# Two usual pairs in place of four ahead of the up projection's seven-product loop

## The chip, the cores and the metric

The kernel runs on one core of a Trainium2 chip. The metric is the device time of one execution in microseconds; lower is better. TensorE (PE) multiplies matrices, VectorE (DVE), ScalarE (ACT) and GpSimd (POOL) do the elementwise work, SyncE (SP) starts most of the transfers. Each engine runs its own instructions in the order written; semaphores connect them.

## The reference

One transformer block and a second one of two layers, for one sequence of 1024 tokens and width 1024. The change lies in the feed-forward part of the first block alone:

```
h2 = rms_norm(x, norm2_g)
up = h2 @ w_up                      # 1024 -> 2 * 2816
up = causal_depthwise_conv(up, ffn_dw_w)     # width 3
gate, val = split(up, 2)
x = x + (silu(gate) * val) @ w_down
```

The 2816 channels are 22 tiles of 128. A tile of the gate and the tile of the value that goes with it are called a pair: 22 pairs, each with 1024 x 256 weights.

## The kernel before

Activations lie transposed, channels on the 128 partitions. A (8 tiles of 128 x 1024, f32) is the normed input of the up projection. TensorE multiplies in a reduced 32-bit type, so each factor is split in a high part (a copy in that type) and a low part (the rest), and each product is three matmuls: high by high, high by low, low by high (lines 253 to 255, 2012 to 2014).

**Usual pairs** (`up_first_pe`, line 1986; UP_FIRST = 4 of them, numbers 0 to 3). `dense_unit` multiplies the unit's weights (WH, WL, 128 x 2048) with the halves HH, HL of the input: 8 row tiles x 2 (gate, value) x 2 halves of the tokens x 3 = 96 matmuls of 512 columns. Pairs 0 and 2 go to the PSUM banks PB, pairs 1 and 3 to TBB and OBB. The input isn't normed by tokens yet, so DVE scales the result by rbx (`scaled`, L2146), then come the copies with the last tap (ScalarE, L2098 and L2100, into G0 and V0), the other taps (`taps_of`, DVE, L2081), silu (ScalarE) and the product gate by value (DVE, L2158), which SP stores to `ub`. The unit's low part is a DVE subtraction (`low_part`, L269), its high part a GpSimd transfer (L3244).

**Pairs in seven products** (`up_pe`, line 1999; pairs 4 to 21). A pair's product is cut in 2 x 2 quarters: weights by row half and gate or value, input by row half and token half. Seven products of sums of quarters (M0 to M6), 4 row tiles x 3 = 12 matmuls each, replace eight: 84 matmuls. For them the kernel needs

- seven *mixes* of the input, made once: sums on GpSimd (mixes 2, 4, 6; `mixed`, L2211, four operations each) or DVE (3 and 5; `mix_sum`, L2055), each with a high part (ScalarE, `mix_high`, L2048) and a low part (DVE, `mix_low`, L2060). They lie in XH and XL; mixes 3 to 6 lie over HH and HL, so they wait until the last usual pair has read these (marks h1, h3, h5 and the pair's end);
- seven *pieces* of each pair's weights: sums on GpSimd (0 to 3 and 6; `piece_sum`, L2203), high parts on ScalarE (`piece_high`, L2066), low parts on DVE (`piece_low`, L2072). Raw weights come by SP (`up`, L2515) to RAW and RAW1 by turns; RAW1 shares memory with rbx;
- combinations of the seven results: m2, a ScalarE copy of M0 (L2126 or L2258), which product 4 waits for; q, r and others on DVE (L2190, L2314). Product 5 waits for q, product 6 for r.

The pairs run as `ffn_up0` (two pairs, 4 and 5, written out), `ffn_up` (a loop of two pairs a round, UP_LOOPS rounds) and `ffn_up_last` (20 and 21). The work that readies pair 4 lies in `up_first_act`, `up_first_dve` and `up_pool`, woven into that of the usual pairs. In `up_first_dve` the order is: mix 0 and 1 low, pair 0, mix 2 low, pairs 1 and 2 with a split each, then sum for mix 3, pieces 0 to 3, sum for mix 5, mix 3 low, scaling of pair 3, mix 4 low, pieces 4 and 5, mix 5 low, q, mix 6 low, r, piece 6, taps of pair 3; then in `up_dve` pieces 0 to 3 of pair 5.

The product that begins a pair waits for its piece 0, and the first pair's for its mixes too:

```
if j:
    pe.e.wait_ge(dve_done, at_mark(pe, "dve", f"w{p}_0", i))
else:
    pe.e.wait_ge(dve_done, at_prev(pe, "dve", f"w{p}_1", i))
    if ph == UP_PHASES[0]:
        pe.e.wait_ge(dve_done, done_in("dve", "ffn_first", f"x{p}"))
```

Beside the loop, 16 *gained* units go through ScalarE: SP loads a unit of later weights to gs (L2559), ScalarE multiplies it by gains (`gain_unit`, L2240, 16 operations), SP stores it to `gu` (L2549). Before, these go with pairs 5 to 20.

Of the kernel before, what the change touches and what calls it, by code (L numbers as in the profile page):

```python
# [41 lines left out]
DIFF_HEADS = 8  # L42
# [27 lines left out]
U_FFN = U_WO + 4  # L70
UP_FIRST = 4
U_DOWN = U_FFN + UP_FIRST
# [11 lines left out]
def build(nc, io, counts, stop=None):  # L84

    made = {"pe": {}, "act": {}, "dve": {}}
    with ExitStack() as ctx:
# [1998 lines left out]
        def up_first_act(act):  # L2086
            e = act.e
# [20 lines left out]
            for p in range(3):  # L2108
                mix_high(act, p)
            for j in range(3):  # L2110
                gate_value(j)
                silu(j)
# [4 lines left out]
            mix_high(act, 4)  # L2117
            e.wait_ge(pe_done, at_mark(act, "pe", "v3"))
            for p in (4, 5):
                piece_high(act, p, 1, UP_FIRST)  # L2120
            mix_high(act, 5)
            gate_value(3)
            e.wait_ge(dve_done, at_mark(act, "dve", "x1"))
# [7 lines left out]
        def up_first_dve(dve):  # L2131
# [33 lines left out]
            mix_low(dve, 2)  # L2165
            low_part(dve, U_FFN + 2)
            scaled(1)
            taps_of(1)
            product(1)
            low_part(dve, U_FFN + 3)  # L2170
            scaled(2)
            taps_of(2)
            product(2)
            mix_sum(dve, 3, "h1")
# [3 lines left out]
            mix_low(dve, 3)  # L2178
            scaled(3)
            mix_low(dve, 4)  # L2180
# [16 lines left out]
            combined("ra_f", 3, "r_f", rb[:, 0, :], rb[:, 0, :], ALU.add)  # L2197
            taps_of(3)

# [5 lines left out]
        def up_pool(pool, high):  # L2205
# [9 lines left out]
            mixed(2)  # L2215
            for n in (U_FFN + 2, U_FFN + 3):
                high(n, 0, io["units"][n:n + 1])
            pool.wait_ge(raw_up[0], 16)
            pool.wait_ge(pe_done, done_in("pe", "ffn_first", "v2"))
            for p in range(4):  # L2220
                piece_sum(pool, p, UP_FIRST)
            for p, name in ((4, "h3"), (6, "v3")):
                pool.wait_ge(pe_done, done_in("pe", "ffn_first", name))
                mixed(p)
# [7 lines left out]
        def up_act(act, ph):  # L2232
            e = act.e

            def gain_unit(j, i):

                e.wait_ge(gain_in, counted(act, i, 32, 16 * j))
                for n in range(2 * KT):
                    part = gs[:, n * P:(n + 1) * P]
                    ins = e.activation(part, part, ACT.Copy, scale=p_(("pre_b", "kvn")[n // KT], n % KT, 1))  # L2240
                ins.then_inc(act_done, act.mark(f"gain_{j}"))

            def body(i):
                for j in range(2):
# [14 lines left out]
                    if build:  # L2259
                        for p in range(3):  # L2260
                            high(p)
                        if first:
                            e.wait_ge(dve_done, done_in("dve", "ffn_first", f"cg_{tag(UP_FIRST - 1)}"))
                            e.activation(G0[:, :], G0[:, :], ACT.Silu).then_inc(act_done, act.mark("si_f"))
                        else:
                            gain_unit(j, i)
# [243 lines left out]
        def ffn_sp(sp):  # L2510
# [11 lines left out]
            def tile(n):  # L2522
# [9 lines left out]
                sp.dma_start(us_in[n % 8][:, :], io["ub"][k][:, half_of(h)]).then_inc(u_in[n % 8], 16)  # L2532

            for j in range(UP_FIRST - 1):
                if j == 2:
                    sp.wait_ge(unit_split, U_DOWN)
                    up(UP_FIRST)
                store(j, V0[:, :], done_in("dve", "ffn_first", f"mu_{tag(j)}"))
            sp.wait_ge(dve_done, done_in("dve", "ffn_first", "sv3"))
            up(UP_FIRST + 1)  # L2540
# [4 lines left out]
            for t in range(UP_FIRST, FF_TILES):  # L2545
                j, r = t % 2, t - UP_FIRST - 1
                if 0 <= r < 2 * DIFF_HEADS:
                    sp.wait_ge(act_done, up_at("act", t, f"gain_{j}"))
                    sp.dma_start(io["gu"][r], gs[:, :]).then_inc(gain_out, 16)  # L2549
                if t < FF_TILES - 1:  # L2550
                    sp.wait_ge(summed, FIRST_SUMS["p6"] + 5 * (t + 1 - UP_FIRST))
                    sp.wait_ge(dve_done, up_at("dve", t, f"w5_{j}"))
                    up(t + 3)
                if r + 1 < 2 * DIFF_HEADS:
                    if t == UP_FIRST:
                        sp.wait_ge(u_out[(t - 1) % 2], 16 * (t // 2))
                    else:
# [999 lines left out]
```

## Time and profile before

| | |
|---|---|
| median of 3 runs | 2693.42 us (2691.63 to 2694.85) |
| the profiled execution | 2696.82 us, span 2695.2 us |
| PE busy | 2647.1 us (98%), 13124 matmuls recorded |
| DVE busy | 1642.8 us (61%) |
| ACT busy | 951.5 us (35%) |
| POOL busy | 466.3 us (17%) |
| chain that ended last | PE 86%, DVE 6%, issue 2% |

Spans of matmuls overlap: each is shown as 0.39 us long, but they start 0.23 us apart. The granted clock is 1.00 at 2.4 GHz and 0.50 at 1.2 GHz. The up projection lies between 502 and 944 us of the span.

### The profile page before, as it was taken

To read this page: it belongs to the slowest core of one execution; us is meant where nothing else is said; L and a number is where in the kernel's file an instruction comes from. 1 tells how busy PE (TensorE), PEld (TensorE's weight loads), DVE (VectorE), ACT (ScalarE), POOL (GpSimd) and SP (SyncE) were. 2 spreads that over 40 slices of the span, in tenths; PEclk is the share of its full clock that TensorE was granted. 3 is DMA by queue.
4 is the path that set the end of the run, shared out by engine and by line. 5 is a ranking of instruction groups with operands and counts; after the bars stand their busy time and mean duration, and the time that the engine had idled before them with its cause. 6 is when DMAs were issued, how large, how long until landed. Compare 5 with 4: busy or idle time off the path is not lost.

```text
span 2695.2 us, 35949 instructions
## 1 busy us (share of the span) xinstructions
PE 2647.1 (98%) x13124; PEld 2139.3 (79%) x13140; DVE 1642.8 (61%) x2211; ACT 951.5 (35%) x1858; POOL 466.3 (17%) x386
## 2 busy tenths in 40 slices
PE   9999989999999999999999999999999999999988
PEld 7767657887888878888888888888877888888877
DVE  8955564688888854245345345354476666666665
ACT  5333341336666633232112112112144444444451
POOL 0899900133333200111000000000000000000000
PEclk9999999999999999999999999999999999999999
DMA  5211113324545564242222222222243222222326
GB/s 194 80 64 62 47 63 141 125 102 166 200 184 197 193 259 148 94 172 79 78 93 78 78 93 78 78 93 78 78 156 131 74 77 78 78 78 78 117 74 224
DMA packets 61993, 307.25 MB, mean 114 GB/s; under 512 B 7776, under 2 KB 8928, under 8 KB 33504
## 3 DMA queue, kind: packets, MB, share of 16 engines
q1 hardware_dynamic: 39200, 191.23, 19.7%
q0 software_dynamic: 10800, 78.65, 8.8%
q10 hardware_dynamic: 11920, 36.38, 3.5%
q8 instruction: 48, 0.79, 0.1%
q14 instruction: 25, 0.20, 0.0%
HBM read 252.75 MB, written 45.09 MB: 111 GB/s over the span
## 4 chain that ended last, share of the span: by engine, by line
PE 86%; DVE 6%; issue 2%; ACT 1%; DMA 1%; SPq 0%; DVEq 0%; ACTq 0%; POOLq 0%
PE OBB L253 10%; PE OBB L255 9%; PE OBB L254 9%; PE PB L253 5%; PE PB L255 5%; PE PB L254 5%; PE TBB L253 4%; PE TBB L255 4%; PE TBB L254 4%; PE TBB L994 3%; PE PB L1043 2%; PE OBB L1110 2%; PE PB L2012 2%; PE PB L2014 2%; PE PB L2013 2%
## 5 line engine op out<-in xcount | busy, mean ns | idle before, releaser
L253 PE MATMUL OBB<-HH,WH 128*128 128x512 f32 x736 | 300.2, 408 | 3.2 <-issue 3.0
L255 PE MATMUL OBB<-HH,WL 128*128 128x512 f32 x736 | 289.4, 393 | 0.0
L254 PE MATMUL OBB<-HL,WH 128*128 128x512 f32 x736 | 289.2, 393 | 0.0
L3244 POOL DMA_DIRECT2D WH<-units x59 | 32.1, 543 | 1181.9 <-PE OBB L253 733.8
L269 DVE TENSOR_TENSOR WL<-RAW,WH 128x2048 fp32r<-128x2048 f32 x75 | 178.1, 2375 | 83.8 <-DMA WH<-units 82.2
L1249 ACT ACTIVATE E<-PB,small 128x128 f32<-128x128 f32 (+3 forms) x192 | 141.1, 739 | 222.8 <-DVE small L1347 213.9
L253 PE MATMUL PB<-HH,WH 128*128 128x512 f32 x528 | 214.2, 406 | 2.8 <-DVE HL L415 1.8
L255 PE MATMUL PB<-HH,WL 128*128 128x512 f32 x528 | 205.8, 390 | 0.0
L254 PE MATMUL PB<-HL,WH 128*128 128x512 f32 x528 | 205.6, 389 | 0.0
L1347 DVE TENSOR_REDUCE small<-PB 128x1 f32<-128x128 f32 (+3 forms) x192 | 138.7, 752 | 62.8 <-PE PB L1061 62.8
L2203 POOL TENSOR_TENSOR WLF<-RAW 128x512 f32<-128x512 f32 x90 | 126.7, 1411 | 225.9 <-PE PB L2014 99.6
L255 PEld LDWEIGHTS OBB<-HH,WL 128*128 128x128 f32 x736 | 139.6, 190 | 31.4
L253 PEld LDWEIGHTS OBB<-HH,WH 128*128 128x128 f32 x736 | 139.7, 190 | 30.7 <-issue 4.0
L254 PEld LDWEIGHTS OBB<-HL,WH 128*128 128x128 f32 x736 | 140.1, 190 | 26.1
L2891 ACT ACTIVATE vr<-OBB,rtok 128x256 f32<-128x256 f32 x32 | 15.3, 477 | 353.2 <-PE OBB L255 353.2
L2405 DVE TENSOR_TENSOR WL<-RAW,WH 128x2048 fp32r<-128x2048 f32 x22 | 51.9, 2358 | 130.2 <-ACT WH L2400 130.1
L3277 POOL TENSOR_TENSOR cacc<-cacc,prod 128x498 f32<-128x498 f32 (+29 forms) x94 | 129.1, 1374 | 0.0
L3266 POOL TENSOR_TENSOR prod<-hc,par 128x498 f32<-128x498 f32 (+29 forms) x94 | 121.5, 1293 | 6.8
L253 PEld LDWEIGHTS PB<-HH,WH 128*128 128x128 f32 x528 | 99.1, 188 | 28.4 <-issue 4.7
L2072 DVE TENSOR_TENSOR WL<-WLF,WH 128x512 fp32r<-128x512 f32 x90 | 102.2, 1140 | 29.2 <-ACT WH L2066 29.2
L254 PEld LDWEIGHTS PB<-HL,WH 128*128 128x128 f32 x528 | 99.2, 188 | 24.5 <-issue 4.5
L255 PEld LDWEIGHTS PB<-HH,WL 128*128 128x128 f32 x528 | 99.1, 188 | 21.2
(477 smaller groups left out, 6413.7 us busy)
## 6 DMA issues: line engine op xcount, KB each, us to landing
RAW<-units SPq DMA_DIRECT2D x81, 1024.0 KB, 4.8
WH<-units POOLq DMA_DIRECT2D x59, 1024.0 KB, 5.2
RAW<-ups SPq DMA_DIRECT2D x18, 1024.0 KB, 4.8
gs<-units SPq DMA_DIRECT2D x16, 1024.0 KB, 7.0
gu<-gs SPq DMA_DIRECT2D x16, 1024.0 KB, 3.9
RAW<-gu SPq DMA_DIRECT2D x16, 1024.0 KB, 4.9
WH<-gu POOLq DMA_DIRECT2D x16, 1024.0 KB, 5.1
ub<-V SPq DMA_DIRECT2D x22, 512.0 KB, 2.6
```

Of the source, the lines that this page charges most:

```text
L253: first = pe.e.matmul(out, wh, xh, start=start, stop=False)
L254: pe.e.matmul(out, wh, xl, start=False, stop=False)
L255: return pe.e.matmul(out, wl, xh, start=False, stop=stop), first
L269: dve.e.tensor_tensor(WL[s][:, :], RAW[:, :], WH[s][:, :].bitcast(F32), ALU.subtract).then_inc(unit_split, 1)
L994: mm = pe.e.transpose(dst[:, c * P:(c + 1) * P], src(b), c_("ident"))
L1043: pe.e.matmul(PB[c][:, b:b + w], q_part[rows, t * P:(t + 1) * P], k_part[rows, b:b + w], start=q_part is qh and k_part is kh, stop=False, ...
L1249: e.activation((E0, E1)[c][:, 0:n], PB[c][:, 0:n], ACT.Exp, bias=small[:, c, t:t + 1], accum_out=small[:, 2 + c, t:t + 1]).then_inc(act_do ...
L1347: e.tensor_reduce(small[:, c, t:t + 1], PB[c][:, 0:(t + 1) * P], AX, ALU.max, negate=True).then_inc(dve_done, dve.mark(f"m{c}_{t}"))
L2072: dve.e.tensor_tensor(piece(WL, p), source, piece(WH, p).bitcast(F32), ALU.subtract).then_inc(dve_done, dve.mark(f"w{p}_{j}"))
L2203: pool.tensor_tensor(piece(WLF, p), raw_quarter(t % 2, a), raw_quarter(t % 2, b), op).then_inc(summed, 1)
L3266: ins = pool.tensor_tensor(prod[:, n % 2, 0:b - a], hc[:, c, a - d:b - d], weight.to_broadcast([P, b - a]), ALU.mult)
L3277: pool.tensor_tensor(cacc[:, c, a:b], cacc[:, c, a:b], prod[:, n % 2, 0:b - a], ALU.add).then_inc(conv_taps, 1)
```

## The change

UP_FIRST goes from 4 to 2: pairs 0 and 1 are made in the usual way, pairs 2 to 21 in seven products; the loop makes two pairs more (UP_LOOPS 8 in place of 7). Marks and waits that named pairs 2 and 3 are written by UP_FIRST. The work of pairs 1 and 2 and of their splits is taken out of the middle of `up_first_dve`, and two unit transfers out of `up_pool`. SP asks for the first raw weights ahead of its first store. The gained units now go with pairs 4 to 19.

```diff
-UP_FIRST = 4
+UP_FIRST = 2
...
             for p in range(3):
                 mix_high(act, p)
-            for j in range(3):
+            for j in range(UP_FIRST - 1):
                 gate_value(j)
                 silu(j)
...
-            e.wait_ge(pe_done, at_mark(act, "pe", "v3"))
+            e.wait_ge(pe_done, at_mark(act, "pe", f"v{UP_FIRST - 1}"))
...
-            gate_value(3)
+            gate_value(UP_FIRST - 1)
...
             product(0)
             mix_low(dve, 2)
-            low_part(dve, U_FFN + 2)
-            scaled(1)
-            taps_of(1)
-            product(1)
-            low_part(dve, U_FFN + 3)
-            scaled(2)
-            taps_of(2)
-            product(2)
             mix_sum(dve, 3, "h1")
...
-            scaled(3)
+            scaled(UP_FIRST - 1)
...
-            taps_of(3)
+            taps_of(UP_FIRST - 1)
...
             mixed(2)
-            for n in (U_FFN + 2, U_FFN + 3):
-                high(n, 0, io["units"][n:n + 1])
             pool.wait_ge(raw_up[0], 16)
-            pool.wait_ge(pe_done, done_in("pe", "ffn_first", "v2"))
+            pool.wait_ge(pe_done, done_in("pe", "ffn_first", f"v{UP_FIRST - 2}"))
             for p in range(4):
                 piece_sum(pool, p, UP_FIRST)
-            for p, name in ((4, "h3"), (6, "v3")):
+            for p, name in ((4, "h3"), (6, f"v{UP_FIRST - 1}")):
...
-                        else:
+                        elif ph == UP_PHASES[1]:
                             gain_unit(j, i)
...
+            sp.wait_ge(unit_split, U_DOWN)
+            up(UP_FIRST)
             for j in range(UP_FIRST - 1):
-                if j == 2:
-                    sp.wait_ge(unit_split, U_DOWN)
-                    up(UP_FIRST)
                 store(j, V0[:, :], done_in("dve", "ffn_first", f"mu_{tag(j)}"))
...
             for t in range(UP_FIRST, FF_TILES):
-                j, r = t % 2, t - UP_FIRST - 1
+                j, r = t % 2, t - UP_FIRST - 2
...
-                if r + 1 < 2 * DIFF_HEADS:
-                    if t == UP_FIRST:
-                        sp.wait_ge(u_out[(t - 1) % 2], 16 * (t // 2))
+                if 0 <= r + 1 < 2 * DIFF_HEADS:
+                    if r < 0:
+                        sp.wait_ge(u_out[(UP_FIRST - 1) % 2], 16 * (UP_FIRST // 2))
```

DVE's order behind the product of pair 0 (the numbers behind the names of tiles are those of their buffers; WL_57 and WL_58 are the two low slots; the difference, before to changed):

```order
 L2158 TENSOR_TENSOR V_156<-G_155,V_156 128x1024
 L2060 TENSOR_TENSOR XL_139<-XF_142,XH_136 128x2048
-L269 TENSOR_TENSOR WL_57<-RAW,WH_55 128x2048
-L2146 TENSOR_TENSOR TBB<-TBB,rbx 128x1024
-L2146 TENSOR_TENSOR OBB<-OBB,rbx 128x1024
...
-L2081 SCALAR_TENSOR_TENSOR V_156<-PB,par,V_156 128x1023
-L2081 SCALAR_TENSOR_TENSOR V_156<-PB,par,V_156 128x1022
-L2158 TENSOR_TENSOR V_156<-G_155,V_156 128x1024
 L2055 TENSOR_TENSOR XF_151<-A 128x2048
 L2072 TENSOR_TENSOR WL_57<-WLF_131,WH_55 128x512 x4
```

Fifteen instructions leave between the low part of mix 2 (L2060) and the sum for mix 3 (L2055); these two now follow each other.

GpSimd's order at the same place, of the changed kernel (line numbers are 8 lower than before; XF_142, XF_152 and XF_154 are the sums of mixes 2, 4 and 6):

```order
L2203 TENSOR_TENSOR XF_142<-A 128x512 x4
L2195 TENSOR_TENSOR WLF_131<-RAW 128x512 x4
L2203 TENSOR_TENSOR XF_152<-A 128x512 x4
L2203 TENSOR_TENSOR XF_154<-A 128x512 x4
L2195 TENSOR_TENSOR WLF_132<-RAW 128x512
L2195 TENSOR_TENSOR WLF_131<-RAW_130 128x512 x4
```

Before, two transfers of unit weights stood between the first two of these rows; nothing else moved here.

## Rows read from the trace of the kernel before

**Rows 1.** The page: PE's busy time; the raw weights' transfers (last column: us to landing).

```profile
PE 2647.1 (98%) x13124; PEld 2139.3 (79%) x13140; DVE 1642.8 (61%) x2211; ACT 951.5 (35%) x1858; POOL 466.3 (17%) x386
...
RAW<-ups SPq DMA_DIRECT2D x18, 1024.0 KB, 4.8
```

**Rows 2.** Busy time by stretch: pair 1, pairs 4, 5 and 6.

```profile
core 0: us, PE busy (x) PEld busy (x) DVE busy (x) ACT busy (x) POOL busy (x), PEclk, DMA share, GB/s
...
526.18:547.94 21.76, 21.76 (x98) 18.02 (x97) 15.15 (x11) 6.27 (x5) 6.46 (x5) 1.00 0.19 54
...
591.46:614.82 23.36, 19.61 (x85) 15.53 (x84) 23.29 (x18) 12.39 (x15) 20.45 (x10) 0.98 0.27 90
614.82:636.97 22.15, 22.15 (x85) 17.93 (x86) 19.98 (x26) 12.46 (x31) 5.38 (x4) 0.86 0.48 189
636.97:656.16 19.19, 19.19 (x86) 15.77 (x85) 16.82 (x19) 13.12 (x31) 6.84 (x5) 1.00 0.49 192
```

**Rows 3.** PE's waits from 590 to 940: us in total, times, longest.

```profile
PE OBB L2012 <- DVE WL L2072: 3.3, 1, 3.3
PE PB L2012 <- DVE WL L2072: 0.5, 1, 0.5
```

**Rows 4.** PE in order of time: start us, us; first products 0 and 4 of pair 5.

```profile
614.82 0.77 PE L2012 MATMUL OBB<-XH,WH 128*128 128x512 f32 x1 [3.28 <-DVE WL L2072]
...
628.80 0.39 PE L2012 MATMUL OBB<-XH,WH 128*128 128x512 f32 x1
```

**Rows 5.** Busy time by stretch, in pair 5; the granted clock is the 0.53.

```profile
619.00:621.00 2.00, 2.00 (x7) 1.54 (x6) 1.86 (x4) 1.54 (x4) 0.57 (x1) 0.53 0.37 150
```

**Rows 6.** DVE in order of time, entry to the seven-product pairs (578 to 616).

```profile
578.67 2.28 DVE L2055 TENSOR_TENSOR XF<-A 128x2048 f32<-128x2048 f32 x1
580.87 6.89 DVE L2072 TENSOR_TENSOR WL<-WLF,WH 128x512 fp32r<-128x512 f32 x4
...
589.89 2.28 DVE L2060 TENSOR_TENSOR XL<-XF,XH 128x2048 fp32r<-128x2048 f32 x1
592.09 1.22 DVE L2146 TENSOR_TENSOR TBB<-TBB,rbx 128x1024 f32<-128x1024 f32 x1
...
596.66 3.48 DVE L2072 TENSOR_TENSOR WL<-RAW,WH 128x512 fp32r<-128x512 f32 x2
600.07 3.39 DVE L2060 TENSOR_TENSOR XL<-XF,XH 128x2048 fp32r<-128x2048 f32 x1
...
603.98 2.78 DVE L2060 TENSOR_TENSOR XL<-XF,XH 128x2048 fp32r<-128x2048 f32 x1
...
607.28 1.18 DVE L2072 TENSOR_TENSOR WL<-WLF,WH 128x512 fp32r<-128x512 f32 x1
...
613.99 2.49 DVE L2072 TENSOR_TENSOR WL<-WLF,WH 128x512 fp32r<-128x512 f32 x4
```

**Rows 7.** DVE in order of time behind pair 0: its product, mix 2's low part.

```profile
540.32 1.22 DVE L2158 TENSOR_TENSOR V<-G,V 128x1024 f32<-128x1024 f32 x1
541.46 2.29 DVE L2060 TENSOR_TENSOR XL<-XF,XH 128x2048 fp32r<-128x2048 f32 x1
```

**Rows 8.** GpSimd in order of time: mix 2's first operation, piece sums, mixes 4, 6.

```profile
522.90 5.48 POOL L2211 TENSOR_TENSOR XF<-A 128x512 f32<-128x512 f32 x1 [18.71 <-DVE A L2139]
...
570.02 5.04 POOL L2203 TENSOR_TENSOR WLF<-RAW 128x512 f32<-128x512 f32 x4 [20.86 <-PE PB L255]
580.82 6.40 POOL L2211 TENSOR_TENSOR XF<-A 128x512 f32<-128x512 f32 x4 [5.76 <-PE OBB L255]
591.70 7.89 POOL L2211 TENSOR_TENSOR XF<-A 128x512 f32<-128x512 f32 x4 [4.48 <-PE OBB L255]
```

**Rows 9.** ScalarE in order of time, in pair 5: m2, a gained unit.

```profile
626.88 0.58 ACT L2258 ACTIVATE m<-OBB 128x512 f32<-128x512 f32 x1
...
628.92 4.79 ACT L2240 ACTIVATE gs<-gs,par 128x128 f32<-128x128 f32 x16
```

More of the change, by code:

```diff
@@ L2235, in gain_unit @@
             def gain_unit(j, i):
-                e.wait_ge(gain_in, counted(act, i, 32, 16 * j))
+                e.wait_ge(gain_in, counted(act, i, 32, 16 * (j - 1)))
                 for n in range(2 * KT):
@@ L2532, in tile @@
                 sp.dma_start(us_in[n % 8][:, :], io["ub"][k][:, half_of(h)]).then_inc(u_in[n % 8], 16)
+            sp.wait_ge(unit_split, U_DOWN)
+            up(UP_FIRST)
             for j in range(UP_FIRST - 1):
-                if j == 2:
-                    sp.wait_ge(unit_split, U_DOWN)
-                    up(UP_FIRST)
                 store(j, V0[:, :], done_in("dve", "ffn_first", f"mu_{tag(j)}"))
-            sp.wait_ge(dve_done, done_in("dve", "ffn_first", "sv3"))
+            sp.wait_ge(dve_done, done_in("dve", "ffn_first", f"sv{UP_FIRST - 1}"))
             up(UP_FIRST + 1)
```

## The prediction

> **What bounds the kernel now.** First the page: TensorE (PE) is busy 98% of the span [rows 1]. So a matmul less is worth time, unless its place is one where PE waits. The profiled execution took 2696.82 us for a span of 2695.2; the median of the runs is 2693.42, 3.4 lower. The differences below are worked out on the profiled span and put on the median. 0.2%, about what a measurement can tell from no change, is 5.4 us.
>
> Next the table by stretch, cut where PE begins a new pair [rows 2]. A usual pair takes 21.76 us. The steady pair of the loop takes 19.19. But the first two pairs in seven products take 23.36 and 22.15, 45.51 together against 38.38 at the steady pace: **7.13 us are lost at the entry**. The list of waits says how [rows 3]: PE stops for 0.5 us before the first pair's last product (WL piece 6 is late) and for 3.3 us before the second pair's first product (WL piece 0). The second wait ends with the row at 614.82; behind it the granted clock is at the 1.2 GHz level, and the 0.53 of the stretch from 619 to 621 says that 2.4 GHz comes back just before 621 [rows 4, 5].
>
> Both waits end with a DVE instruction, so the third view is DVE's order of time. From 578.67, the sum for mix 3, DVE has no gap that counts until 614.6, when it ends the low part of the next pair's piece 0, the first of the four from 613.99 [rows 6]. PE starts at 614.82. **At the entry DVE is the bound, not PE.**
>
> **The change, part by part.**
>
> *Matmuls.* Two usual pairs leave (2 x 21.76 = 43.52 us of PE), two steady loop pairs come (2 x 19.19 = 38.38): **-5.14 us** on PE [rows 2]. This is the whole of what the change can give where nothing waits; it is also 12 matmuls a pair, 24 in all, at about 0.22.
>
> *The entry moves forward.* The first seven-product pair now wants to start at 547.94, where pair 2 started, in place of 591.46: 43.5 us earlier. What must be done by DVE, ScalarE and GpSimd for it is the same work (seven mixes of the activations, seven pieces of the weights). Before, mixing had the time of three usual pairs behind pair 0; now of one.
>
> *DVE.* Its chain starts after pair 0's product (540.32, 1.22 long) and the low part of mix 2 (541.46, 2.29), so at 543.75 by the rows of before [rows 7]. Before, GpSimd was idle there. Now it has gone on from mix 2 (522.90 + 5.48 + 3 x 1.26 = 532.1) to the four piece sums (5.04 us, to 537.1), then waits for h3, which PE gives at 526.18 + 4 x 2.72 = 537.06, and makes mix 4 until 542 to 543. DVE's product and mix 2's low part each meet one of its operations.
>
> What meeting costs: alone, DVE's 128x512 low part takes 0.68 (starting 0.60 apart, as in four in 2.49 us); beside GpSimd's mix 4 four of them took 6.89, so 1.1 us more each, and GpSimd's own four took 6.40 in place of 5.04 [rows 6, 8]. They take turns. I take 0.4 for the product and 1.1 for the low part: the chain starts at **545.2**.
>
> From there before: the sum for mix 3 starts at 578.67, PE's second pair at 614.82, **36.15 us** later [rows 4, 6]. Of these, 8.7 are turns given to GpSimd: 4.4 in the four low parts, 2.2 in the two at 596.66, 1.1 at 600.07, 0.5 at 603.98 and 0.5 at 607.28. Now mix 4 is over before the chain begins; mix 6 (4 operations) still waits for PE to end the last usual pair, at 548, as it did at 591.70 [rows 8], and with piece sum 6 it meets five DVE operations: 5 x 1.1, and 0.5 + 0.5 at the end as before, 6.5. That is 2.2 less. 36.15 - 2.2 = 33.95, and the second pair starts at 545.2 + 33.95 = **579.15**. The first one takes 579.15 - 547.94 = 31.2 us in place of 23.36: **+7.85**.
>
> Where PE waits in it: products 0 to 2 follow (their low parts end from 548.0 on, PE loses 0.1 to 0.6), then product 3 at about 556.3 needs mix 3's low part. DVE reaches it after three low parts, the sum for mix 5 and four or five turns: 548.0 (piece 0) + 3 x 0.6 + 2.2 + 2.2 + 4 x 1.1 = 558.6, or 559.7 with a fifth turn. So a wait of 2.5 to 3.6 us that the trace of before does not have, since there the same low part, begun at 589.89, ended at 592.2, and its product came at 591.46 + 3 x 2.74 = 599.7. What follows (WL 4, the combination q, WL 6) is DVE's again: some 2 us in small waits, then 3.4 before the second pair.
>
> *The second pair.* From PE's start at 614.82 to the end of m2 (626.88 + 0.58) pass 12.6 us: DVE's taps, ScalarE's silu, then the copy m2 that product 4 waits for [rows 4, 9]. Before, it was ready 1.3 us ahead of the product (628.80), because the slow clock held PE. Now, if the clock falls again, the pair takes 22.15 as before; if it doesn't, product 4 waits for m2 anyway and the pair takes 12.6 + 0.1 + 3 x 2.74 = 20.9. I take 21.6: **-0.55**. For the same reason a slow clock after the wait at product 3 costs nothing: the products behind it wait for DVE.
>
> *What costs nothing.* DVE loses two 2.28 splits, two scalings, taps and products; ScalarE two sets of copies and silu: all lay beside the two pairs that go. GpSimd loses two DMA issues. The raw weights of the first loop pair are asked for when pair 1's unit is split, while pair 0 is still multiplied (it ends at 526.18); they land some 4.8 us later [rows 1], before the sums want them (532.1). Raw slot 1 shares memory with rbx and is loaded behind the last scaling, as before; that scaling (from about 559) now lies 20 us ahead of the second pair's start, as 592.09 lay 22.7 ahead of 614.82, and the load needs some 5 of them. The 16 gained units move to tiles 4 to 19, so all are in the loop; each loop pair carries one as before (16 groups of 16 short ScalarE activations, 4.79 us [rows 9]), and ScalarE is at 13 of 19 us per pair [rows 2], which covers it. The two further loop pairs carry one each like their neighbours. The last pair's end and the down projection are not touched.
>
> **The sum:** -5.14 + 7.85 - 0.55 = +2.16, **+2.1 us**: 2693.4 + 2.1 = **2695.5**. Ends of the unknown terms: with no turn given to GpSimd at all, the chain is 36.15 - 8.7 = 27.45 from 543.75, the second pair starts at 571.2, and the sum is (23.3 - 23.36) + (20.9 - 22.15) - 5.14 = -6.5; with all 8.7 and both meetings in front in full (chain from 546), it starts at 582.15 and, with a slow second pair, the sum is -5.14 + 10.85 = +5.7. Rows of before show turns being taken at all but one place, so I stay near the upper half.
>
> *A rule against a row.* At 522.90 a GpSimd operation of 1.3 us took 5.48: DVE ran two low parts of 2.28 back to back and GpSimd got nothing between them [rows 8]. At 580.82 they alternate. If DVE keeps going at 548 as it did at 522.90, it does three low parts, the sum and mix 3's low part (five operations) without a turn. GpSimd's five operations then fall on later ones, and on the scaling of the two PSUM tiles, which at 592.09 took 1.22 beside GpSimd's mix [rows 6, 8], as a product of that size took alone [rows 7]. That saves about 4 turns, 4.4 us: -2.3 in place of +2.1.
> The Trainium skill (SBUF — State Buffer, SBUF: two separate sides) has the pair of ports as an exclusive lock that whoever starts first holds for the whole instruction. By that rule the one that waits gets its turn at the instruction's end and the sum is +2.1; the row at 522.90 doesn't agree, those from 580.82 on do.
>
> **The rivals.**
> A. *DVE keeps GpSimd out* as just told: 2693.4 - 2.3 = 2691.1. For it: 522.90. Against: 580.87, 596.66, 600.07 [rows 6].
> B. *The entry costs no more than before* (7.13 lost, as now), because ScalarE or the matmuls and not DVE set it: the whole -5.14 stays, 2688.3. For it: PE is 98% busy. Against: DVE is at 23.29 of 23.36 us in that stretch [rows 2]. If it even shrinks, the time is down to 2686.9, the -6.5 above.
> C. *Slower: two waits, two falls of the clock, both paid.* The wait of 2.5 to 3.6 us before product 3 is about as long as the one that sent the clock to 1.2 GHz. If it falls there and DVE's low parts are not what the next products wait for, its cost of 2.96 (22.15 against 19.19) is added to +2.1, and with one or two more turns lost the sum is +5.7: 2699.1. It decides where the wait is like the one of 3.3 us [rows 3].
> D. *The change doesn't shorten PE's work*: excluded by the order of instructions (192 matmuls less ahead of the loop, one loop round more of 168, written as a loop count).
>
> **How the numbers follow.** The forecast (2693.5 to 2697.5) 0.52; A 0.22; B 0.08; C 0.18. Times run from 2690.5, between A and B, to 2699.5, just above C. Beyond -5.4 lies half of B and the tail of A: faster 0.06. Beyond +5.4 lies the upper half of C and a tail: slower 0.12. Within: 0.82.
>
> **What would show it.** In the changed kernel's table by stretch: a first seven-product pair of about 31 us (right) or 23 (B), 27 (A); DVE without a gap from 540 to 590; a PE wait of 2.5 to 3.6 us in front of product 3, ended by XL of mix 3, and one of about 3.4 in front of the second pair, ended by WL piece 0; a steady pair still 19.19. A first pair under 28 us, or a steady pair off 19.19, would make the prediction wrong.

## The result and the profile after

The changed kernel takes **2700.96 us** (median of 7 runs, 2699.0 to 2705.42); the kernel before, on the same chip, 2692.7 (7 runs, 2690.29 to 2698.05). The ratio is 1.0026, its 95% interval 1.0017 to 1.0035. Run again beside r1 to r4 it gave 2701.21 and a ratio of 1.0021 [1.0011, 1.0031]. So the change costs 6.6 to 8.3 us where +2.1 was forecast, and the time lies above the range. The profiled execution took 2700.96 us for a span of 2699.3.

What of it was foreseen? First the busy time by stretch, cut where PE begins a new pair, as [rows 2]: the first three seven-product pairs (columns as there).

```profile
548.55:579.22 30.67, 22.94 (x85) 17.43 (x85) 30.60 (x22) 15.29 (x17) 18.59 (x10) 0.89 0.20 69
579.22:600.56 21.34, 21.29 (x84) 16.86 (x85) 20.71 (x26) 8.71 (x15) 5.88 (x4) 0.92 0.27 99
600.56:619.75 19.19, 19.19 (x85) 15.77 (x84) 16.77 (x18) 12.51 (x30) 6.81 (x5) 1.00 0.50 192
559.20:566.00 6.80, 5.85 (x14) 4.56 (x15) 6.80 (x7) 3.69 (x4) 0.00 (x0) 0.50 0.38 126
```

The first pair takes 30.67 in place of 23.36, with DVE busy for 30.60 of it; the second 21.34; then 19.19, the steady pace of before. The last row is a stretch of 6.8 us at 1.2 GHz (granted clock 0.50); it begins at 559.2, in the last us of the wait for product 3. PE's waits from 548 to 602, as [rows 3]:

```profile
PE OBB L2012 <- DVE WL L2072: 3.3, 1, 3.3
PE PB L2012 <- DVE XL L2060: 3.1, 1, 3.1
PE PB L2012 <- DVE WL L2072: 1.9, 2, 1.4
```

The second row is the new wait, for the low part of mix 3; the first is the one before the second pair. DVE in order of time, as [rows 6, 7] (lines behind 2166 are 8 to 10 lower in the changed kernel):

```profile
540.54 1.66 DVE L2158 TENSOR_TENSOR V<-G,V 128x1024 f32<-128x1024 f32 x1
542.12 3.37 DVE L2060 TENSOR_TENSOR XL<-XF,XH 128x2048 fp32r<-128x2048 f32 x1
545.42 2.28 DVE L2055 TENSOR_TENSOR XF<-A 128x2048 f32<-128x2048 f32 x1
547.62 5.79 DVE L2072 TENSOR_TENSOR WL<-WLF,WH 128x512 fp32r<-128x512 f32 x4
553.34 3.38 DVE L2055 TENSOR_TENSOR XF<-A 128x2048 f32<-128x2048 f32 x1
556.64 3.36 DVE L2060 TENSOR_TENSOR XL<-XF,XH 128x2048 fp32r<-128x2048 f32 x1
...
568.40 2.77 DVE L2060 TENSOR_TENSOR XL<-XF,XH 128x2048 fp32r<-128x2048 f32 x1
...
578.39 1.89 DVE L2072 TENSOR_TENSOR WL<-WLF,WH 128x512 fp32r<-128x512 f32 x3
```

GpSimd beside it, as [rows 8] (mix 4; mix 6; piece sum 6; the sums for the next pair):

```profile
537.31 6.04 POOL L2203 TENSOR_TENSOR XF<-A 128x512 f32<-128x512 f32 x4
548.10 6.47 POOL L2203 TENSOR_TENSOR XF<-A 128x512 f32<-128x512 f32 x4 [4.75 <-PE OBB L255]
554.52 3.33 POOL L2195 TENSOR_TENSOR WLF<-RAW 128x512 f32<-128x512 f32 x1
567.24 8.02 POOL L2195 TENSOR_TENSOR WLF<-RAW 128x512 f32<-128x512 f32 x4 [9.39 <-DMA RAW<-ups]
```

Chain and second pair stand where they were forecast, to within 0.3: the chain starts at 545.42 (forecast 545.2), the second pair at 579.22 (579.15). PE's last matmul of the up projection (the last XH matmul) starts at 945.70, before at 943.72: **+1.98, near the +2.1 of the sum**. But the kernel ends 4.1 later in this pair of profiles, and the medians lie 8.3 apart here and 6.6 in the repetition. The next loss stands 3 us behind that matmul, where the down projection starts (UH is the high part of its input, us_in the raw input from `ub`, L2395 and L2405 the low part of its first weights). The kernel before, PE in order of time:

```profile
943.72 0.39 PE L2014 MATMUL TBB<-XH,WL 128*128 128x512 f32 x1
945.87 0.50 PE L253 MATMUL PB<-UH,WH 128*128 128x512 f32 x1 [1.76 <-DVE WL L2405]
```

The changed kernel:

```profile
945.70 0.39 PE L2014 MATMUL TBB<-XH,WL 128*128 128x512 f32 x1
948.92 0.79 PE L253 MATMUL PB<-UH,WH 128*128 128x512 f32 x1 [2.84 <-DVE WL L2395]
```

The first UH matmul comes 3.22 us behind the last XH matmul in place of 2.15, and its 0.79 instead of 0.50 shows the slow clock, which falls at 948.4 for 3.4 us. DVE's WL waits for ScalarE's WH, and WH stands in ScalarE's order behind the copies of four us_in tiles. The changed kernel:

```profile
940.00 0.63 ACT L2375 ACTIVATE UH<-us_in 128x512 fp32r<-128x512 f32 x1 [5.78 <-DMA us_in<-ub]
942.75 1.99 ACT L2375 ACTIVATE UH<-us_in 128x512 fp32r<-128x512 f32 x3 [2.12 <-DMA us_in<-ub]
944.64 1.90 ACT L2390 ACTIVATE WH<-RAW 128x2048 fp32r<-128x2048 f32 x1
```

The kernel before:

```profile
938.03 0.63 ACT L2385 ACTIVATE UH<-us_in 128x512 fp32r<-128x512 f32 x1 [5.78 <-DMA us_in<-ub]
939.70 1.98 ACT L2385 ACTIVATE UH<-us_in 128x512 fp32r<-128x512 f32 x3 [1.04 <-DMA us_in<-ub]
```

Counted from the last XH matmul, the first tile is copied at the same time in both (5.7 us ahead). The second is copied 2.95 ahead instead of 4.02: its transfer lands 1.1 us later (2.97 ahead for 4.05), though SP issues it at the same time (9.83 ahead in both). What else the transfers meet in the last 10 us of the up projection, in the DMA view: the kernel before (933.7 to 943.7),

```profile
q1 hardware_dynamic: 1572, 3.13, 95.8%
issues: line engine op xcount, KB each, median us to landing
us_in<-ub SPq DMA_DIRECT2D x12, 256.0 KB, 5.7
```

and the changed one (935.7 to 945.7; per queue: packets, MB, share of 16 engines):

```profile
q1 hardware_dynamic: 1468, 2.95, 88.4%
q8 instruction: 1, 0.02, 0.6%
issues: line engine op xcount, KB each, median us to landing
us_in<-ub SPq DMA_DIRECT2D x11, 256.0 KB, 6.9
```

One packet of the instruction queue, a load of 16 KB of code, lies in it, and holds one of the 16 DMA engines for 0.96 us (0.6% of 160). It stands 5.5 us ahead of the last XH matmul. In the kernel before, the nearest one stands 7.5 us behind it, where no tile is late.

### The profile page after: what moved, and what is told of

Its sections match the earlier page's. It is cut to its first block, busy times and chain, and to the rows that moved or that the text cites. A ratio compares the mean times of both kernels' runs of the same rounds, so it can differ in the third digit from the quotient of the medians.

```text
span 2699.3 us, 36075 instructions
## 1 busy us (share of the span) xinstructions
PE 2647.6 (98%) x13116; PEld 2136.4 (79%) x13116; DVE 1653.5 (61%) x2231; ACT 960.7 (36%) x1878; POOL 477.2 (18%) x394
## 4 chain that ended last, share of the span: by engine, by line
PE 73%; DVE 5%; issue 1%; ACT 1%; DMA 1%; POOL 0%; ACTq 0%; SPq 0%; DVEq 0%; POOLq 0%
PE OBB L253 8%; PE OBB L255 8%; PE OBB L254 8%; PE PB L253 4%; PE PB L255 4%; PE PB L254 4%; PE TBB L255 4%; PE TBB L253 4%; PE TBB L254 4%; PE PB L1043 2%; PE PB L2012 2%; PE OBB L1110 2%; PE PB L2014 2%; PE PB L2013 2%; PE TBB L994 2%
## 5 line engine op out<-in xcount | busy, mean ns | idle before, releaser
L253 PE MATMUL OBB<-HH,WH 128*128 128x512 f32 x720 | 293.5, 408 | 3.0 <-issue 3.0
L255 PE MATMUL OBB<-HH,WL 128*128 128x512 f32 x720 | 283.0, 393 | 0.0
L254 PE MATMUL OBB<-HL,WH 128*128 128x512 f32 x720 | 282.7, 393 | 0.0
L253 PE MATMUL PB<-HH,WH 128*128 128x512 f32 x496 | 201.7, 407 | 2.0 <-DVE hc L918 1.1
L255 PE MATMUL PB<-HH,WL 128*128 128x512 f32 x496 | 193.4, 390 | 0.0
L254 PE MATMUL PB<-HL,WH 128*128 128x512 f32 x496 | 193.2, 390 | 0.0
L2195 POOL TENSOR_TENSOR WLF<-RAW 128x512 f32<-128x512 f32 x100 | 140.7, 1409 | 238.1 <-PE PB L2014 112.1
L2395 DVE TENSOR_TENSOR WL<-RAW,WH 128x2048 fp32r<-128x2048 f32 x22 | 51.9, 2360 | 131.0 <-ACT WH L2390 130.9
L2072 DVE TENSOR_TENSOR WL<-WLF,WH 128x512 fp32r<-128x512 f32 x100 | 113.8, 1143 | 29.6 <-ACT WH L2066 29.6
L2012 PE MATMUL PB<-XH,WH 128*128 128x512 f32 x280 | 111.5, 398 | 5.0 <-DVE XL L2060 3.1
L253 PEld LDWEIGHTS PB<-HH,WH 128*128 128x128 f32 x496 | 93.1, 188 | 26.9 <-issue 4.8
```

Of the source, the lines that this page charges most:

```text
L253: first = pe.e.matmul(out, wh, xh, start=start, stop=False)
L254: pe.e.matmul(out, wh, xl, start=False, stop=False)
L255: return pe.e.matmul(out, wl, xh, start=False, stop=stop), first
L2012: pe.e.matmul(bank(j, n), wh, XH[p][:, k, :], start=p < 4 and k == 0, stop=False, skip_group_check=True)
L2072: dve.e.tensor_tensor(piece(WL, p), source, piece(WH, p).bitcast(F32), ALU.subtract).then_inc(dve_done, dve.mark(f"w{p}_{j}"))
L2195: pool.tensor_tensor(piece(WLF, p), raw_quarter(t % 2, a), raw_quarter(t % 2, b), op).then_inc(summed, 1)
```

## The experiments

Two theories. **Entry:** DVE and its turns with GpSimd (one of its operations let in ahead of DVE's) bound the entry, as the prediction says. **Code load:** the change shortened PE's code, so that the load of one of its blocks now falls on the first us_in tiles; this delays them, PE waits longer and the clock falls. Rivals: the two profiles differ by luck; or the gained units, which now end a pair earlier, have moved something. All stretches of the profiles together, in us (table of my readings: starts of PE's first products; "third copy" is where ScalarE starts to copy the third us_in tile, "load" the start of the nearest code load, both from the last XH matmul):

|  | first pair | second pair | third copy | last XH to first UH | last XH to last UH | clock falls there | load |
| --- | --- | --- | --- | --- | --- | --- | --- |
| before | 23.36 | 22.14 | -3.35 | 2.15 | 242.95 | no | +7.5 |
| r5 before again | 23.36 | 21.34 | -3.34 | 2.15 | 244.02 | yes | +9.1 |
| r8 | 23.62 | 21.99 | -4.25 | 1.24 | 242.01 | no | +6.8 |
| r10 | 23.37 | 22.00 | -3.82 | 1.68 | 242.46 | no | -2.6 |
| **r12** | 23.36 | 21.39 | **-2.53** | **2.96** | **245.08** | yes | **-5.2** |
| changed | 30.67 | 21.34 | -2.27 | 3.22 | 244.79 | yes | -5.5 |
| r1 changed again | 30.65 | 21.98 | -2.52 | 2.98 | 244.83 | yes | -5.1 |
| r4 | 29.85 | 22.02 | -2.88 | 2.61 | 244.49 | yes | -5.4 |
| r6 | 30.71 | 21.97 | -2.93 | 2.57 | 244.45 | yes | -5.5 |
| r7 | 26.26 | 21.79 | -2.36 | 3.12 | 245.26 | yes | -4.9 |
| r11 | 31.17 | 21.35 | -2.64 | 2.86 | 244.70 | yes | -5.2 |
| **r9** | 30.67 | 21.39 | **-3.43** | **2.08** | **242.97** | no | **-13.2** |
| r13 | 28.50 | 21.34 | -4.13 | 1.45 | 242.22 | no | -12.9 |

With a load at -4.9 to -5.5 the third copy starts at -2.3 to -2.9, in all seven; without one, at -3.3 to -4.3, in all six. The landings say the same without the copies: the third tile lands 2.6 to 3.4 us behind the first with such a load, 1.4 to 2.4 without. r2 and r3, which change the order of these copies, stand apart below; by the landings they agree (r2 with a load at -6.1: 2.8; r3 without: 1.6).

**r1, the changed kernel again, and r2, r3: the start of the down projection.** r2 makes only the first us_in tile's copy stand ahead of the first unit's weights on ScalarE, and takes that unit's low part forward on DVE; r3 does the same to the kernel before. The diff of r2:

```diff
-                        for k in range(4):
+                        tile_high(act, 0, 0)
+                        down_high(act, 0)
+                        for k in range(1, 4):
                             tile_high(act, 0, k)
-                        down_high(act, 0)
...
-                            low(1)
+                            down_low(dve, 0)
...
-                    low(4 if build else 2)
+                    low(4 if build else 1)
                     if not build:
-                        low(3)
+                        low(2)
...
-                        down_low(dve, 0)
+                        low(3)
```

> The changed kernel once more, against the one before. Theory 1: of the difference, 2.0 us arise at the entry to the seven-product pairs and are in every execution; the rest arises at the start of the down projection, where PE waits for the first weights' low part (2.84 us against 1.76) and the clock falls behind it, and it depends on how late the second activation tile lands; then the profile shows the entry as before (second seven-product pair at about 578.6), the last seven-product matmul at 945.7, and the wait at the start of the down projection again between 1.7 and 3.3 us; ratio 1.002 to 1.003. Rival: the entry itself varies by microseconds from run to run; then the second pair starts elsewhere than 578.6 by over 1 us.

> The changed kernel, with the first down-projection weights split behind the first activation tile in place of the fourth. Theory 1 (some 2.6 us or more of the loss lie at this place): PE's wait there goes from 2.8 us to under 1, the clock stays at 2.4 GHz, and the time falls by 2.5 to 5 us against the changed kernel, to 2696 to 2698.5. Rival (the loss lies at the entry, the place here costs nothing or a wait moves to the second tile): less than 1.5 us gained.

> The same edit on the kernel before (four usual pairs). Theory 1: its wait there was 1.76 us and the clock did not fall, so it gains 1.2 to 2.2 us, clearly less than the changed kernel does. Rival: it gains as much as the changed one, so the place doesn't explain the difference between the two.

Measured: r1 2701.21 (9 runs), r2 2701.29, ratio 1.0021 [1.0012, 1.0031], r3 2695.59, 1.0008 [0.9999, 1.0017]; before beside them 2694.64 (31 runs). r1's up projection as a whole begins 2.3 us later than in the first profile of the changed kernel, so its second pair at 581.47 isn't the rival's case: counted from the last matmul of the row sums (at 511.63, in place of 509.31) it starts after 69.84 us in place of 69.91. Its second pair takes 21.98, with no fall of the clock in it. PE waits there for m2, because DVE's low part in front of it met a GpSimd operation (1.69 us in place of 0.69):

```profile
584.78 1.69 DVE L2072 TENSOR_TENSOR WL<-RAW,WH 128x512 fp32r<-128x512 f32 x1
595.15 0.50 PE L2012 MATMUL OBB<-XH,WH 128*128 128x512 f32 x1 [2.46 <-ACT m L2248]
```

In r2 and r3 the first UH matmul does come 0.23 us behind the last XH matmul. But PE's wait moved to the 49th UH matmul, the first of the fifth us_in tile, in r2

```profile
959.65 0.76 PE L253 MATMUL PB<-UH,WH 128*128 128x512 f32 x1 [2.61 <-DVE UL L2381]
```

and the last UH matmul is at 244.57, in r3 at 243.71 (before 242.95). A miss. This wait isn't for the input, which had landed 15 us earlier, but for DVE, which has the taps of the last pair and the second unit's low part to make first:

```profile
956.61 2.29 DVE L2396 TENSOR_TENSOR WL<-RAW,WH 128x2048 fp32r<-128x2048 f32 x1 [0.58 <-ACT WH L2391]
958.81 2.49 DVE L2381 TENSOR_TENSOR UL<-us_in,UH 128x512 fp32r<-128x512 f32 x4
```

So DVE is a second bound some 14 us behind the last XH matmul, and an earlier first UH matmul alone gains nothing. In the kernel before PE waits there too, for 0.27 us.

**r4, pair 0's gate and value ahead of mix 2 on ScalarE**

```diff
-            for p in range(3):
+            for p in range(2):
                 mix_high(act, p)
             for j in range(UP_FIRST - 1):
                 gate_value(j)
                 silu(j)
+            mix_high(act, 2)
```

> The changed kernel, with ScalarE's copies and silu of pair 0 ahead of the high part of mix 2, which waits for GpSimd until 532.3. If DVE sets the entry: it no longer stands idle from 529.7 to 535.3 but to about 531, its chain to the second seven-product pair starts 3.5 to 4.4 us earlier, less 1 to 2 us of turns with GpSimd's mix 4, and the second pair starts at 575 to 577 in place of 578.6: 2 to 3.5 us gained in all. If ScalarE or the matmuls set it: the second pair stays within 0.5 us of 578.6 and nothing is gained.

Measured: 2698.57 (11 runs), 1.0015 [1.0006, 1.0024]. DVE's taps of pair 0 come over 4 us earlier, and the sum for mix 3 at 541.75 in place of 545.42; the second pair at 577.76, only 1.5 earlier (575 to 577 was expected). DVE and GpSimd in r4:

```profile
541.75 3.37 DVE L2055 TENSOR_TENSOR XF<-A 128x2048 f32<-128x2048 f32 x1
545.04 6.90 DVE L2072 TENSOR_TENSOR WL<-WLF,WH 128x512 fp32r<-128x512 f32 x4
```

```profile
537.41 10.56 POOL L2204 TENSOR_TENSOR XF<-A 128x512 f32<-128x512 f32 x4
```

Mix 4, which was over when the chain began, now takes turns with it: the sum takes 3.37 for 2.28, the four low parts 6.90 for 5.79. An earlier chain gives back 2.2 of the 3.7 us won. PE's new wait fell from 3.1 to 2.4.

**r5, the kernel before again; r6, mix 3's low part first; r7, without mix 6's sum; r8, mix 3's sum on GpSimd in the kernel before**

```diff
# r6
-            mix_sum(dve, 5, "h5")
             mix_low(dve, 3)
+            mix_sum(dve, 5, "h5")
...
# r7
+                    if p == 6:
+                        ins = pool.memset(XF[p][:, k, :], 0.0)
+                    else:
...
# r8
-            mix_sum(dve, 3, "h1")
...
-            for p, name in ((4, "h3"), (6, "v3")):
+            for p, name in ((3, "h1"), (4, "h3"), (6, "v3")):
```

> The kernel before, unedited, once more. Open is whether its quick start of the down projection (first UH matmul 2.15 us behind the last XH matmul, no fall of the clock there) is its habit or one profile's luck. Theory 1 (the change has cost 1.1 us at the start of the down projection): again 2.1 to 2.2 us, last XH to last UH matmul 242.9 to 243.0. Theory 2 (that stretch is the same in both kernels and differs from run to run): 2.6 to 3.2 us, 244.5 to 244.9. Both expect total to last XH matmul 434 (436.4 in the changed kernel), the second pair 22.14 us with a fall, and a ratio of 1.000.

> The changed kernel with mix 3's low part ahead of the sum for mix 5 on DVE. Theory DVE-bound entry: the wait of 3.5 us in front of product 3 goes (mix 3's low part ends about 3.3 us earlier), the fall of the clock at 559 with it, but DVE's chain is as long as before, so mix 5's low part is no earlier, the wait moves behind product 3, and the second pair starts at 579.0 to 579.5 behind a wait as long or longer: total as the changed kernel, 2701. Rival (the wait in front of product 3 and the fall of the clock behind it are what costs): second pair 2 to 3.5 us earlier, total 2698.

> The changed kernel; GpSimd's sum for mix 6 is left out (its tile is set to zero, so product 6 is of zeros). Theory turns: GpSimd's four reading operations at 567 and DVE's instructions no longer take turns; four turns of 1.1 us go, and the second pair starts 3.8 to 4.4 us earlier, at about 575; total 2697. If setting to zero takes turns just as a sum does, nothing changes (579.2). Rival (DVE's chain is long of itself, turns are nothing): 579.2 as well, but then DVE's rows beside GpSimd's are as short as those alone.

> The kernel before with the sum for mix 3 made by GpSimd (four operations behind the piece sums) and not by DVE. Theory DVE-bound entry: 2.28 us leave DVE's chain in front of the second seven-product pair, up to four turns come in (4.4 us) if GpSimd works beside DVE; GpSimd idles from 575 to 581 while DVE scales pair 2, so I expect one or two: second seven-product pair 0 to 2 us earlier (614.8 to 612.6), total 2691.5 to 2693.5. If the entry is not DVE's, no change at all.

Before beside them 2694.71 (33 runs). r5: 2695.56, 1.0004 [0.9995, 1.0014], and the wait of 2.15 once more. But the last UH matmul is at 244.02, between the figures of the two theories: here the clock fell without a load near. So r5 gives the price of one fall there: 241.87 us from first to last UH matmul in place of 240.80, 1.07. (The first 48 matmuls alone take 1.57 more; 0.4 of that goes where PE otherwise waits for the fifth tile.) r6: 2700.28, 1.0022 [1.0013, 1.0031]. PE's waits from 548 to 608 in r6:

```profile
PE PB L2012 <- DVE WL L2072: 5.8, 2, 5.3
PE OBB L2012 <- DVE WL L2072: 3.0, 1, 3.0
PE OBB L2012 <- ACT m L2248: 2.4, 1, 2.4
```

The wait for mix 3 is gone; a larger one stands one product later, in front of product 4, and the first pair takes 30.71. The rival, that this one wait is what costs, falls. r7: 2697.16, 1.0005 [0.9996, 1.0014]; the second pair starts 26.26 us behind the first, 4.4 less. GpSimd and DVE in r7:

```profile
548.88 1.92 POOL L2204 MEMSET XF<- 128x512 f32 x4 [4.63 <-PE OBB L255]
```

```profile
548.52 2.48 DVE L2072 TENSOR_TENSOR WL<-WLF,WH 128x512 fp32r<-128x512 f32 x4
```

Beside clearing, the four low parts take 2.48, as alone; beside the sum they took 5.79. Four turns gone, 4.4 us gone, all of it on PE's path: the entry theory is shown at its price of 1.1 a turn. The Trainium skill (SBUF — State Buffer, Who interferes with whom) says that a DVE instruction with two SBUF inputs contends with a GpSimd one that reads SBUF, not with one that only writes it; these two rows agree. r8: 2694.16, 0.9997 [0.9988, 1.0006], a first pair of 23.62, where a second pair up to 2 us earlier was expected: GpSimd's eight operations took 14.89 us and the turns ate the 2.28 saved.

**r9, PE's code moved; r10, the same in the kernel before; r11, r4 with mix 3's sum on GpSimd.** r9 (r10 has 225 for 129):

```diff
-            pe.e.wait_ge(act_done, done_in("act", "mix", "cum_lo"))
+            for _ in range(129):
+                pe.e.wait_ge(act_done, done_in("act", "mix", "cum_lo"))
```

> The changed kernel with 128 waits more in PE's program, all for a mark long reached, at a place where PE stands still for 3.9 us anyway (129 to 133 us). They do no work; they move the later code of PE against the blocks in which it is loaded. In all five traces of the changed kernel or its variants a load of 16 KB of code lies 5.5 us ahead of the last XH matmul, in the middle of the transfers of the first us_in tiles; in all traces of the kernel before it lies 7.5 us behind it. Theory code load (it delays the second us_in tile, and with it the down projection): with the load 7 or 15 us earlier the first UH matmul comes 2.15 us behind the last XH matmul again, the last UH matmul 242.9 to 244.0 behind it in place of 244.5 to 245.3; total about 2700.0. Rival (the landing depends on something else, as the gained units, which now end a pair earlier): 2.6 to 3.2 and 244.5 to 245.3 as before. Entry unchanged in both, 579.2.

> The kernel before with 224 such waits at the same place, which take longer than the stall there (a loss of 3 to 10 us ahead of the up projection is possible; the stretches behind it are what is compared). Theory code load: where they bring the load of PE's code to about 5 us ahead of the last XH matmul, the first UH matmul comes 2.6 to 3.2 us behind the last XH matmul in place of 2.15; where they bring it elsewhere (two waits may share an instruction or not), 2.15 stays. Rival (gained units): 2.15 wherever the load lies.

> The changed kernel with pair 1's taps on DVE ahead (as r4) and the sum for mix 3 made by GpSimd. Theory DVE-bound entry: 2.28 us leave DVE's chain, but GpSimd, four operations longer, works beside more of DVE's instructions; the kernel before gained nothing by the same edit (r8). Second pair at 575.5 to 577.8 against 577.76 in r4; total 2696.5 to 2698.5. If turns eat all of it, as r4.

Before beside them 2694.94 (25 runs). **r9: 2698.52, 1.0016 [1.0007, 1.0025]**, by idle instructions alone 3.6 over its neighbours of before where r1 was 6.6 over its own. The totals scatter too much to size this (the intervals overlap; by the ratios it is 1.3 us); the stretch from the last XH to the last UH matmul does: 242.97 for 244.83, 1.9 us. The DMA view of r9's last 10 us of the up projection, and ScalarE's copies:

```profile
q1 hardware_dynamic: 1540, 3.08, 97.7%
issues: line engine op xcount, KB each, median us to landing
us_in<-ub SPq DMA_DIRECT2D x12, 256.0 KB, 5.6
```

```profile
940.59 0.63 ACT L2376 ACTIVATE UH<-us_in 128x512 fp32r<-128x512 f32 x1 [6.04 <-DMA us_in<-ub]
941.93 1.98 ACT L2376 ACTIVATE UH<-us_in 128x512 fp32r<-128x512 f32 x3 [0.71 <-DMA us_in<-ub]
```

The load is gone from the stretch (it had lain 5 to 6 us ahead in the changed kernel's profiles, and 5.7 to 9.1 behind in those of the kernel before, not always 7.5), the tiles land after 5.6 us, the second copy starts 4.1 ahead of the last XH matmul, and the clock holds. The entry is that of the changed kernel (30.67). r10: 2698.45, 1.0013 [1.0004, 1.0022]; its 3.5 us over the kernel before were lost at the place of the waits (8.28 us between two of PE's matmuls there, before 4.25), and its load came at -2.6, behind the sixth tile: first UH matmul at 1.68. There the load shows all the same: the seventh us_in tile lands 1.81 us behind the sixth, where from the third tile to the eighth neighbours else land 0.64 to 0.76 us apart, in every profile. But this tile isn't wanted yet, and nothing waits for it. r11 (the taps that r4 brings forward are pair 0's, not pair 1's as its expectation says): 2702.65, 1.0028 [1.0018, 1.0038]. A miss: GpSimd's twelve operations took 26.46 us, so its last mixes came late, PE waited 5.5 us for one copy, and the second pair came at 579.28, 31.17 us behind the first.

**r12, the load brought to the same place in the kernel before (277 for 225 in the loop); r13, r4 and r9 together**

> The kernel before with 276 waits more at the same place as in r10 (224 of them moved the load of PE's code from 7.5 to 9 us behind the last XH matmul to 2.6 ahead of it, with some 4 us lost at the place of the waits). 52 waits more are 26 instructions, so 3 us: the load at 5 to 6 us ahead of the last XH matmul, as in the changed kernel. Theory code load: second us_in tile late, the third ScalarE part of it at 2.9 to 2.3 us ahead of the last XH matmul in place of 3.35, first UH matmul at 2.6 to 3.2 in place of 2.15, a fall of the clock behind it, last UH matmul at 244.5 to 244.9 in place of 242.9 to 244.0. Rival (gained units or anything else of the changed kernel): 2.15, as without the load.

> The changed kernel with both: pair 0's gate and value copies and silu ahead of mix 2's high part on ScalarE (r4) and PE's code moved by 128 waits (r9). Theory (both costs are real and add up): second pair at 577.8, first UH matmul 2.1 us behind the last XH matmul, no fall of the clock there; total 2701.2 - 2.6 - 2.7 = 2696. Rival (the totals differ by the clock's falls elsewhere, not by these): 2698.5 as each alone.

Before beside them 2694.95 (21 runs). r12, PE and the DMA view (939.1 to 949.1):

```profile
952.02 0.80 PE L253 MATMUL PB<-UH,WH 128*128 128x512 f32 x1 [2.58 <-DVE WL L2406]
```

```profile
q1 hardware_dynamic: 1560, 3.11, 94.8%
q8 instruction: 1, 0.02, 0.6%
```

The kernel before, with its own gained units and pairs, starts its down projection as late as the changed one once the load stands at -5.2: 2.96, slow clock, 245.08. The rival falls. Its total, 2702.47, 1.0025 [1.0016, 1.0034], holds 6.8 us lost at the place of the waits (11.09 there against 4.25), and isn't a measure of the load. r10 has the same kind of edit with the load elsewhere, and no late start: the idle instructions by themselves don't make one. **r13: 2695.23, 1.0001 [0.9992, 1.001]**: the second pair 28.50 us behind the first, 1.45 at the handover, and the time of the kernel before. Against the changed kernel the second pair starts 2.2 us sooner behind the first, which starts 0.7 sooner (counted from the row sums), and the last UH matmul is 2.6 nearer, 5.4 in all, and the median is 6.0 under r1's; here the intervals, [0.9992, 1.0010] and r1's [1.0011, 1.0031], stand apart. That both costs are real, this shows. That they add up it shows less well: with r4's edit alone the first pair took 29.85, and of the 1.35 less in r13, 1.1 is one turn fewer in the four low parts (5.80 for 6.90); as far as these runs tell, that is chance. No version beat the kernel before.

## Why the prediction was wrong

- *Matmuls, -5.14*: right. The steady pair is 19.19, the usual one 21.76, and the two that left are gone.
- *DVE's chain and the first pair, +7.85*: right, with its mechanism. Product and mix 2's low part met mix 4 at 0.44 and 1.08 us (taken: 0.4 and 1.1). Five turns followed (three in the low parts, one in the sum for mix 5, one in mix 3's low part), then 0.5 and 0.5: 6.5, the figure taken. The first pair took 30.67 for 31.2, since it began 0.6 later than pair 2 had (PE waited 0.54 for its first low part). The instructions of DVE that left ahead of the chain are sixteen, not fifteen; no sum used the number. r7 shows that the turns are paid.
- *The wait before product 3, 2.5 to 3.6*: it is 3.1, the one before the second pair 3.3.
- *The second pair, -0.55*: in this profile 21.34 against 22.15. But both kernels take either: the kernel before 22.0 and 22.1 where the clock is low for 6.8 us, 21.3 and 21.4 where it is for 3.4 (r5, r12), the changed one 21.3 and 21.4 (r9) too, and 21.98 in r1 without a fall. The term was one profile's draw, not a gain of the change, and the 20.9 that the prediction gave to a pair at full clock was seen nowhere: in r1 and r6, without a fall, m2 came 1 us later, behind a turn given to GpSimd. Without the term the sum is +2.7. From the last matmul of the row sums, which stands early in pair 0, to the last XH matmul the changed kernel takes 436.5 us in the mean of its profile, r1, r2 and r9, the kernel before 433.8 in that of its own, r3, r5, r10 and r12: +2.7. That this one pair of profiles shows +1.98, so near +2.1, is in part luck.
- *"The last pair's end and the down projection are not touched"*: **this step failed**. The instructions there are the same, but 192 matmuls and their weight loads fewer lie in front of them, and the loads of PE's code come at other places. One load falls on the first us_in tiles, which the sum had at nothing: 0.8 to 1.1 us more of waiting (r1, the changed kernel) and a fall of the clock that costs about 1.07. Taking it out took 1.9 us from the stretch (r9); putting it in made the kernel before's as long as the changed one's (r12).
- *Rival A* (GpSimd kept out): no; every one of the five turns was given. *Rival B*: no. *Rival C* came nearest to the time and with the wrong mechanism (nor does its +5.7 follow from its own terms, +2.1 and 2.96 and a turn of 1.1): two falls of the clock in the entry do happen (559.2 and 579.7), but cost nothing there, since the products behind them wait for DVE, as the prediction had it; the fall that is paid is a third one, 350 us later. *D* stays excluded.

The entry makes +2.7 of the 6.6 between r1 and the kernel before, the load 1.9 against the kernel before's own profile, but only 0.8 against r5, where the clock fell by itself. So 2 to 3 us aren't settled. r13 points the same way: from the row sums to the last UH matmul its profile takes 675.7 us, the kernel before 677.3, and yet its median isn't lower. Behind the last UH matmul the 301st instruction of ScalarE starts after 850.4 to 850.7 us in the changed kernel and its variants (r11: 850.1), after 849.8 to 850.1 in the kernel before and its own; why isn't known. Later the clock falls at other lengths from run to run (6.8 or 3.4 us at one place in profiles of both kernels), which moves single times by more than that.

Of the code load, the Trainium skill (Runtime: NRT & Kernel Launch, Instruction fetch mechanics) says that code comes in blocks of 16 KiB by a queue of its own and that crossing a block is mostly hidden. The trace agrees in the size, 16384 bytes for each of the instruction queue's packets. That it is hidden held for PE itself here, whose matmuls ran through; not for the data that shared the DMA engines.

## What to carry to other kernels

An edit that adds or takes instructions of PE moved the code loads behind it here (the change itself, r9, r10, r12). Where a stage starts on transfers with little to spare, look in both traces for the instruction queue in the last 10 us ahead of it; a few idle instructions in a place where the engine stands still move it, and so tell that cost from the edit's own.

Where DVE and GpSimd both read SBUF, count their meetings and price each at about one GpSimd operation (1.1 us here; alone such an operation takes 1.26): starting DVE earlier, or handing it less, gains little while the other engine's operations are still to come (r4, r8, r11). And take no term from one profile's clock: repeat the kernel before as often as the changed one.

## What the runs showed of the hardware

- A code load of one packet, 0.89 to 0.98 us of one of 16 DMA engines, went with a third 256 KB tile that landed 2.6 to 3.4 us behind the first instead of 1.4 to 2.4, and with a first UH matmul 2.57 to 3.22 us behind the last XH matmul instead of 1.24 to 2.15, in all seven profiles in which it stood 4.9 to 5.5 us ahead of the latter. At -2.6 it fell on the seventh tile, 1.1 us late without cost to PE; at +7 or at -13 no tile was late. By which way so short a packet costs as much as its own length or more wasn't tried.
- The clock fell at the end of the wait at the handover or just behind it in all of those, in one of the four profiles of the kernel before or its variants without the load there (r5), and in neither of the changed kernel's. A fall of 3.4 us cost 1.07 up to the last UH matmul (r5 against the profile before) and nothing visible at the entry.
- GpSimd's clearing of a tile gave DVE's reads no turn to wait for (1.92 for four, DVE's 2.48 as alone), where its sums cost 1.1 each. Which of two waiting engines goes next isn't fixed: the same four low parts met four operations in r4 (6.90) and three in r13 (5.80).
